# Cached keys of a decoder layer: from TensorE transposes in the attention to VectorE transposes during the projections

## What is computed

```python
xn = rmsnorm(x, norm_mix_pre)
q, k, v, u_a, v_a = project(xn, w_in)              # 4 heads; k and q are 2 x 64 per head
pk = cache_k[l][page_table]                        # 8 sequences x 8 pages x 128 keys x 4 heads x 128
pv = cache_v[l][page_table]
o_b = diff_head_out(attend(q, k, v, lam), ...)     # softmax(q1 k1) - lam * softmax(q2 k2), both + bias
o_a, vn = spatial_gate(u_a, v_a, ...)              # u * (W_s LayerNorm(v) + b) in chunks of 128
x = x + rmsnorm(concat(o_b, o_a) @ w_out, norm_mix_post)
f, new_buf = conv_ffn(rmsnorm(x, norm_ffn_pre), ...)
x = x + rmsnorm(f, norm_ffn_post)
```

## Time and profile before

| | before |
|---|---|
| median of 3 runs (lowest to highest) | 1375.17 us (1374.22 to 1375.6) |
| profiled execution, span of its trace | 1374.4 us |
| PE busy | 1351.8 us |
| DVE busy | 703.4 us |
| ACT busy | 461.7 us |
| projections | 46 to 282.3 us |
| attention | 282.3 to 457.2 us |

### The profile page before, as it was taken

One profiled execution on the slowest core, in us unless ns is written; L12 is line 12 of the kernel. 1 busy time (PEld: TensorE's weight loads), 2 busy tenths in 40 slices (PEclk: granted clock), 3 DMA queues, 4 the chain that ended last, 5 costly groups with the idle time before them and its releaser, 6 DMA issues.

```text
span 1374.4 us, 22383 instructions
## 1 busy us (share of the span) xinstructions
PE 1351.8 (98%) x8642; PEld 1216.2 (88%) x8642; DVE 703.4 (51%) x1175; ACT 461.7 (34%) x783; POOL 169.7 (12%) x323
## 2 busy tenths in 40 slices
PE   7999999999999999999999999999999999999998
PEld 6999999966667788899898989898989898999986
DVE  6333412166778564554545464646364545364555
ACT  6321012056666643343131313132313232322332
POOL 2254000021212221120000000000000000000003
PEclk9999999999999999999999999999999999999999
DMA  8202123256673633132020202011111102020117
GB/s 267 63 31 66 31 70 104 76 178 187 197 209 146 221 103 120 54 108 77 16 76 15 76 15 70 22 61 31 61 31 40 52 15 76 15 73 19 47 47 134
DMA packets 93658, 113.43 MB, mean 83 GB/s; under 512 B 6477, under 2 KB 65526, under 8 KB 93590
## 3 DMA queue, kind: packets, MB, share of 16 engines
q1 hardware_dynamic: 90457, 105.52, 24.5%
q0 software_dynamic: 992, 3.54, 1.6%
q10 hardware_dynamic: 2140, 3.46, 0.7%
HBM read 97.28 MB, written 14.69 MB: 81 GB/s over the span
## 4 chain that ended last, share of the span: by engine, by line
PE 93%; DVE 2%; issue 1%; ACT 1%; DMA 1%; SPq 1%; POOL 0%; POOLq 0%; DVEq 0%; ACTq 0%
PE PS L2383 38%; PE PS L2094 17%; PE PS L2448 16%; PE PS L2326 7%; PE PS L2187 2%; PE PS L2149 2%; PE PS L2210 2%; PE PS L2463 2%; PE PS L2478 2%; DMA x_in<-in_x_prompt_dram 1%; PE PS L2256 1%; PE PS L2233 1%; PE PS L2079 1%; PE PS L2317 1%; PE PS L2175 1%
## 5 line engine op out<-in xcount | busy, mean ns | idle before, releaser
L2383 PE MATMUL PS<-act_lo,wu_hi 128*128 128x364 f32 (+1 forms) x1056 | 346.5, 328 | 0.0
L2383 PE MATMUL PS<-act_hi,wu_lo 128*128 128x364 f32 (+1 forms) x1056 | 346.1, 328 | 0.0
L2383 PE MATMUL PS<-act_hi,wu_hi 128*128 128x364 f32 (+1 forms) x1056 | 346.0, 328 | 0.0
L2383 PEld LDWEIGHTS PS<-act_hi,wu_hi 128*128 128x128 f32 x1056 | 198.6, 188 | 0.5
L2383 PEld LDWEIGHTS PS<-act_lo,wu_hi 128*128 128x128 f32 x1056 | 198.2, 188 | 0.4
L2383 PEld LDWEIGHTS PS<-act_hi,wu_lo 128*128 128x128 f32 x1056 | 198.4, 188 | 0.0
L1854 DVE TENSOR_TENSOR y_acc<-y_acc,PS 128x512 f32<-128x512 f32 x162 | 111.1, 686 | 116.1 <-PE PS L2448 116.1
L2448 PE MATMUL PS<-wd_hi,g_hi 128*128 128x512 f32 x324 | 130.2, 402 | 0.0
L2448 PE MATMUL PS<-wd_lo,g_hi 128*128 128x512 f32 x324 | 128.0, 395 | 0.0
L2448 PE MATMUL PS<-wd_hi,g_lo 128*128 128x512 f32 x288 | 114.0, 396 | 0.0
L1239 ACT CAST g_hi<-conv 128x1088 fp32r<-128x1088 f32 x21 | 23.1, 1102 | 245.8 <-PE PS L2448 189.7
(11 more groups left out here) (286 smaller groups left out, 2371.4 us busy)
## 6 DMA issues: line engine op xcount, KB each, us to landing
wu_raw<-in_w_up_dram SPq DMA_DIRECT2D x44, 512.0 KB, 3.9
vpage<-in_cache_v_dram SPq DMA_DIRECT2D x64, 256.0 KB, 3.0
kpage<-in_cache_k_dram SPq DMA_DIRECT2D x60, 256.0 KB, 3.0
wd_raw<-in_w_down_dram SPq DMA_DIRECT2D x22, 512.0 KB, 5.3
w_raw<-in_w_in_dram SPq DMA_DIRECT2D x20, 512.0 KB, 4.7
x_in<-in_x_prompt_dram SPq DMA_DIRECT2D x8, 512.0 KB, 7.8
wo_raw<-in_w_out_dram SPq DMA_DIRECT2D x8, 512.0 KB, 6.0
x_res<-in_x_prompt_dram SPq DMA_DIRECT2D x8, 512.0 KB, 4.4
```

What stands on the lines that cost most here:

```text
L2383: mm = nc.tensor.matmul(PS[:, 3 * half + c, 0:kept(c)], a[:, half, k, :], b[:, k, KEPT[c]], start=(j == 0), stop=(j == len(parts) - 1))
```

## The change

- Pages of keys are loaded two at a time (a pair, 32 of them) during the projections, by SP, into one of two places (k_tok0, k_tok2). SP waits for the turn that freed the place.
- DVE turns a pair with one instruction in 32 x 32 blocks into k_tok1 (`turn_pair`, L1542), after the pair is loaded and after all earlier pairs have been stored (there is one k_tok1).
- ACT issues the store of k_tok1 to a DRAM tensor keys_t, 4 KB from each partition (`store_pair`, L961). It waits for the turn.
- Seven sets of 5, 5, 5, 5, 5, 4 and 3 pairs are spread over the jobs of groups va1 to q1. A set's loads stand in SP's queue behind the weights of the group after the one in which it is turned.
- In the attention SP loads units of turned keys (four DMAs each, of 32 partitions, in runs of 1 KB) into kt directly, in three places and one first place. `turn_key` and both `take_keys` are gone; `smp_scores` reads its keys and writes its scores in runs of 32.
- The page table is loaded at the start; some semaphores are shared.

```diff
+    PAIR_SETS = [range(0, 5), range(5, 10), range(10, 15), range(15, 20), range(20, 25), range(25, 29), range(29, 32)]
+    TOK_OF = [2 * (n % 2) if n < 25 else 0 for n in range(NPAIR)]
+    PAIR_AT = [jobs_of(k + 1)[j * len(jobs_of(k + 1)) // len(pairs)] for k, pairs in enumerate(PAIR_SETS) for j in range(len(pairs))]
...
+        def load_pair(n):
+            b = TOK_OF[n]
+            if tok_uses(n):
+                sp.wait_ge(ktok_turned, max(m for m in range(n) if TOK_OF[m] == b) + 1)
+            else:
+                sp.wait_ge(nrm_ready, STEPS)
+            for a in range(2):
+                at_page = page_index(n // 2, 2 * (n % 2) + a)
+                page = sp.value_load(pages[0:1, at_page:at_page + 1], min_val=0, max_val=n_pool - 1)
+                sp.dma_start(k_tok[b][:, a, :], cache_k[0, bass.ds(page, 1)].rearrange("a t h d -> t (a h d)")).then_inc(slot_loaded[b], 16)
...
         for p in range(4, 2 * len(GROUPS)):
             sp.wait_ge(w_lo_ready, p - 1)
             load_w(sp, p)
+            if p % 2 == 1 and p // 2 - 2 < len(PAIR_SETS):
+                for n in PAIR_SETS[p // 2 - 2]:
+                    load_pair(n)
...
         def load_keys(u):
-            pr, c, b2 = unit(u)
-            for p in range(4):
-                n = 4 * u + p
-                if n >= 8:
-                    sp.wait_ge(kturn_ready, n - 7)
-                at_page = NPAGE * (2 * pr + b2) + 4 * c + p
-                page = sp.value_load(pages[0:1, at_page:at_page + 1], min_val=0, max_val=n_pool - 1)
-                sp.dma_start(kpage[u][:, p, :], cache_k[0, bass.ds(page, 1)].rearrange("a t h d -> t (a h d)")).then_inc(kp_loaded[u % 2], 16)
+            if u == 1:
+                sp.wait_ge(kt_loaded[0], 64)
+            if u >= 4:
+                sp.wait_ge(sscore_ready, 2 * (u - 3) + 2)
+            for j in range(4):
+                src = bass.AP(keys_t, (2 * u * 4 * 32 * 4 + j) * 256, [[4 * 256, 32], [32 * 4 * 256, 8], [1, 256]])
+                dst = kt[u][32 * j:32 * j + 32].rearrange("a n i p h t -> a (n i) (p h t)")
+                sp.dma_start(dst, src).then_inc(kt_loaded[kt_place(u)], 16)
...
+        def store_pair(n):
+            act.wait_ge(ktok_turned, n + 1)
+            dst = keys_t[n].rearrange("i d j c -> (i d) (j c)")
+            act.dma_start(dst, k_tok[1][:].rearrange("p a c -> p (a c)")).then_inc(ktok_stored, 16)
...
             if kind in ON_ACT and n >= STEPS:
                 take_job(n)
+            if n in PAIR_AT:
+                store_pair(PAIR_AT.index(n))
...
+        def turn_pair(n):
+            b = TOK_OF[n]
+            dve.wait_ge(slot_loaded[b], 48 + 32 * (tok_uses(n) + 1))
+            if n >= 1:
+                dve.wait_ge(ktok_stored, 16 * n)
+            blocks = k_tok[b][:].rearrange("p a (h j c) -> p j (a h) c", h=H, c=32)
+            turned = k_tok[1][:].rearrange("p a c -> p (a c)").rearrange("p (j n t) -> p j n t", j=4, t=32)
+            nc.vector.transpose(turned, blocks).then_inc(ktok_turned, 1)
...
             if n == len(jobs) - 1:
                 ahead()
+            if n in PAIR_AT:
+                turn_pair(PAIR_AT.index(n))
             if kind in ON_ACT:
                 continue
...
         def smp_scores(j):
-            for i in range(2):
-                pe.wait_ge(kt_ready[i], j + 1)
+            pe.wait_ge(kt_loaded[kt_place(u)], 64 * ((u - 1) // 3 + 1 + (kt_place(u) == 0)))
...
             for h in range(H):
-                mm = nc.tensor.matmul(PS[32 * h:32 * h + 32, SMP_BANK, ks], qp[:, 2 * pr + b2, h, :], kt[:, u % 2, h, ks],
+                out = PS[32 * h:32 * h + 32, SMP_BANK, ks].rearrange("r (p i t) -> r i p t", p=2, t=32)
+                mm = nc.tensor.matmul(out, qp[:, 2 * pr + b2, h, :], kt[u][:, j % 2, :, :, h, :],
                                       start=(j % 4 == 0), stop=(j % 4 == 3))
...
-            for n in keys_of(i):
-                turn_key(n)
```

More of the change, by code:

```diff
@@ L142, in _program @@
     far_min = keep.put("far_min", [P, 4, 2])
-    keep.put("spare", [P, P - 8])
+    pages = keep.put("pages", [1, NB * NPAGE], I32)
+    keep.put("spare", [P, P - 8 - NB * NPAGE])
     gain = keep.put("gain", [P, D])
@@ L238, in _program @@
     lo_place = Region(ACT_BYTES, 2 * ACT_BYTES)
-    kt = lo_place.put("kt", [P, 2, H, 512])
-    kpage1 = lo_place.put("kpage1", [P, 4, 512])
+    kt_a, kt_b, kt_mid = (lo_place.put(n, [P, 2, 4, 2, H, 32]) for n in ("kt_a", "kt_b", "kt_mid"))
     prob0 = lo_place.put("prob0", [P, 2, SEQ])
@@ L333, in own_step @@
         eng.wait_ge(step, steps[id(step)])
-    x_loaded = [sem(f"x_loaded{i}") for i in range(3)]
+    slot_loaded = [sem(f"slot_loaded{i}") for i in range(3)]
     gain_loaded = sem("gain_loaded")
@@ L514, in _program @@
     sbias_loaded = sem("sbias_loaded")
[L515 removed]
     sel_loaded = sem("sel_loaded")
[L517 to L518 removed]
+    ktok_turned = sem("ktok_turned")
+    ktok_stored = sem("ktok_stored")
+    kt_loaded = [sem(f"kt_loaded{i}") for i in range(3)]
     vp_loaded = [sem(f"vp_loaded{i}") for i in range(2)]
@@ L609, in unit, with page_index @@
         return u // 4, u // 2 % 2, u % 2
+    def page_index(u, p):
+        pr, c, b2 = unit(u)
+        return NPAGE * (2 * pr + b2) + 4 * c + p
     SMP_BANK, AT_BANK, PV_BANK, OWN_BANK = 7, 1, 3, 6
@@ L617, in _program, with jobs_of, tok_uses, kt_place @@
     ZERO_STEP = [8, 16, 28, 32]
-    def keys_of(i):
-        return range(2 * i, 2 * i + 2) if i < 2 else range(4, 8) if i == 2 else range(2 * i + 2, min(2 * i + 4, 4 * 2 * NB))
+    NPAIR = NB * NPAGE // 2
+    PAIR_SETS = [range(0, 5), range(5, 10), range(10, 15), range(15, 20), range(20, 25), range(25, 29), range(29, 32)]
+    TOK_OF = [2 * (n % 2) if n < 25 else 0 for n in range(NPAIR)]
+    def jobs_of(g):
+        return [n for n, job in enumerate(jobs) if job[1] == g]
+    PAIR_AT = [jobs_of(k + 1)[j * len(jobs_of(k + 1)) // len(pairs)] for k, pairs in enumerate(PAIR_SETS) for j in range(len(pairs))]
+    def tok_uses(n):
+        return TOK_OF[:n].count(TOK_OF[n])
+    def kt_place(u):
+        return max(u - 1, 0) % 3
     ring, ring_taken = [], []
@@ L1747, in _ @@
                     out_norm(i - 3)
-            for n in keys_of(i):
-                if n % 2 == 1 and n not in (3, 5):
-                    take_keys(n)
             if i == 0:
@@ L2202, in turn_out @@
             mm.then_inc(ot_ready, 1)
-        def turn_key(n):
-            u, p = n // 4, n % 4
-            if p == 0:
-                pe.wait_ge(kp_loaded[u % 2], 64 * (u // 2 + 1))
-            pe.wait_ge(*ring_free("key", n))
-            for h in range(H):
-                mm = nc.tensor.transpose(PS[:, ring_bank("key", n), P * h:P * h + P], kpage[u][:, p, P * h:P * h + P], ident[:])
-            mm.then_inc(kturn_ready, 1)
         def own_scores():
```

87 lines of the change are left out of this document (31 added, 56 removed).

## The result

The changed kernel takes 1406.93 us (median of 4 runs, 1405.57 to 1408.69) against 1374.76 before (median of 4, 1374.22 to 1375.6); the ratio is 1.0232, 95% interval 1.0219 to 1.0244. It is slower by 32 us, where I had forecast 15.

The account below looks back on a forecast made before the run. PE was taken as the bound, busy in 1351.8 of 1374.4 us. Stalls of 29.6 us in the projections less 15.0 gained in the attention gave +14.6, hence 1390 us, range 1370 to 1410.

Parts of the forecast that it names:

- case B: Rival, chance 0.18: worse than 1376 to 1402; period near 5.6 us or more (1400), or the clock falls (1402 to 1412).
- case A: The forecast itself, chance 0.56: chain delays PE by 16 to 35 us, attention gives 11 to 20; 1376 to 1402.
- The turn and the period: Projections' chain: 1.2 us a turn on DVE; with hand-overs, store landing and load contention 5.0 us a pair, bounds 4.0 to 5.6.
- The idle time of the projections: PE stalls from turns and stores: 17.2 us up to k0, 7.2 by job 38, 5.2 before krow; 29.6 in sum.
- the granted clock under full after the stalls: Sign listed as showing the prediction wrong: PE's clock below its higher level after stalls; nothing for it in the sum.
- The attention's 15.0 us: Gain in the attention from dropping PE's transposes of cached key pages: 15.0 us summed by step, bounds 11 and 20.
- steps 0 to 3: First narrow attention steps: gain 2.8 us, four times 1.02 less 1.3 for the later-requested second unit of keys.
- Steps 8 to 11: Narrow attention steps: gain 3.5 us, after 1.1 lost because sample scores wait for the softmax of the scores before.
- 16 to 19: Narrow attention steps: the same 3.5 us gain as in steps 8 to 11.
- the wide ones: Wide attention steps 20 to 27, paced by a loop of DVE and ACT: gain about 1.1 us.
- C: Rival, chance 0.14: faster, the projections' chain costs less than the attention gives; 1368, or 1358 to 1371.
- D: Rival, chance 0.12: attention becomes bound by its key loads to 32 partitions, losing part of its gain; 1395 to 1400.

Follow-up runs that it names:

- experiment 3: Changed kernel with the turns of pairs 5 to 9 moved inside DVE's LayerNorm rounds instead of behind them; 1387.71 us, ratio 1.0095 to the kernel before.
- experiment 6: Changed kernel with sets of 5, 8, 0, 5, 5, 5, 4 pairs, the 8 turned inside the LayerNorm rounds; 1377.24 us, ratio 1.0007 to the kernel before.
- experiment 9: experiment 7 with the second loading place usable up to pair 29 and sets of 5, 8, 0, 6, 5, 6, 2; 1365.75 us, ratio 0.9927.
- experiment 5: Changed kernel storing only half of each turned pair (2 KB from each partition); 1396.90 us, ratio 1.0156 to the kernel before.
- experiment 4: Changed kernel with turned pairs going to two places in turn up to pair 24, each with its own semaphore; 1387.29 us, ratio 1.0086 to the kernel before.
- Experiment 8: experiment 1 with the second unit of keys given its own place and requested earlier, as in experiment 7; 1363.64 us, ratio 0.9912 to the kernel before.
- experiment 2: experiment 1 with each key load going to all 128 partitions, 2 KB each, instead of 32 partitions, 8 KB each; 1366.72 us, ratio 0.9931.
- experiment 7: experiment 6 with the second unit of keys given its own place and requested at the last projection group's first job; 1374.15 us, ratio 0.9987.
- experiment 1: Changed kernel with no pair loaded, turned or stored in the projections; attention loads cache blocks as they lie; 1367.01 us, ratio 0.9932 to the kernel before.

## Why the prediction was wrong, point by point

The direction was right and its mechanism too; the size was off by a factor of two, because one term was left out of the sum and one mis-sized. The sum said +14.6 us and the traces show +31.9. Of the 17.3 between, 9.7 are busy time of PE behind the stalls that the sum had at nothing, 7.2 are missing from the attention's gain, and 0.4 is idle time. The range of 1370 to 1410 held 1407 only by the half of case B that it took in; case A's own, 1376 to 1402, did not.

**The turn and the period: right.** 1.24 us for a turn (1.2 taken), 5.14 us a pair (5.0 taken). The parts were not quite: most stores land in 2.8 to 3.1, and the 0.7 that I spread over every pair is a single landing of 6 to 7 us in a set, beside the weights. The "11 percent" of the period in which DVE runs was wrong: 1.2 of 5.0 us is 24.

**The idle time of the projections: right.** 29.6 us worked out, 30.0 measured, at the places named: job 27 7.4 (5.7 forecast), k0 10.0 (11.5), jobs 37 and 38 6.5 (7.2), krow 6.2 (5.2), and none in q0, q1 and v. That the sum is right to 0.4 us is in part luck, since its terms miss by 0.7 to 1.7 in both directions; and nearly half of the third, the wait of 3.1 before job 37, ended with ACT's copy of the last u job, not with the key copy that I had traced. Experiments 3, 6 and 9 moved the turns, and most of the waits went, experiment 5 gave the slope.

**The price of the stalls in clock: left out of the sum.** I had it only as rival B, for one job behind each of three stalls, up to 12 us; it belonged in the forecast, since the forecast itself made the gaps. Measured: 9.7 us more of busy time, 8.8 of it the clock. The term is "29.6 us", which should have been 39.3. "TensorE: Matmul & The Clock Gate" of the Trainium skill, section "Why this matters for your kernels", had warned of idle gaps, and the trace now agrees: the granted clock is 0.94 over the projections, with rows of 0.50 us a matmul behind four of the stalls. A run that keeps PE busy through its stalls was not tried, so this split of the loss rests on the trace, while experiments 3, 4 and 9 show only that clock and stalls go together (0.987, 0.989 and 0.994 over their spans, 0.981 for the change). The prediction named "the granted clock under full after the stalls" among the signs that it was wrong, and it is the sign that came, with PE's wait for keys.

**The attention's 15.0 us: mis-sized, 7.8 measured.** By the starts of DVE's mixing in each step, before and after, the delay goes from 37.5 us at step 0 to 41.8 at step 2, 38.5 at step 11, 36.9 at step 19, 35.9 at step 24 and 32.05 at step 31. So steps 0 to 3 did not give 2.8: 2.2 are gained ahead of the first mixing (39.7 at the end of the projections, 37.5 there) and 3.6 lost behind it. The wait of 4.5 us for the second unit did that, where I had allowed 1.3; its unit is requested at 322.9 and used at 331.1, 8.2 us later and not 6, with two more units requested right behind it. Steps 8 to 11 gave 2.4 (3.5 forecast), 16 to 19 1.2 (3.5), 28 to 31 3.7 (4.1), and the wide ones 1.9 in all (1.1). Experiment 8 puts what the wait cost at 2.8 to 3.4 us and leaves 11 to 12 of the 15. The wait for the sample exponential is the one that I had named for the middle blocks, at the price that I had named (1.05 us). What I had not counted is the clock behind it in step 16: from the start of the products to the first transpose behind them PE takes 3.82 us there (405.24 to 409.06) and 2.59 in step 8 (362.21 to 364.80). That is the 1.2 us by which steps 16 to 19 gave less than 8 to 11. The 1.1 us by which both blocks fall short besides may stand in waits that the kernel before does not have: PE waits for o_nrm, that is for DVE, 0.97 and 0.90 us in steps 11 and 12, and the same in 19 and 20:

```profile
380.12 0.68 PE L2210 MATMUL PS<-v_all,at_sb 128*128 128x128 f32 x4 [0.97 <-DVE o_nrm L1584]
...
384.22 0.91 PE L2210 MATMUL PS<-v_all,at_sb 128*128 128x128 f32 x6 [0.90 <-DVE o_nrm L1584]
```

I had taken it that PE sets the pace in narrow steps with the transposes gone as with them. No run separates these waits, so this last part stays open.

**The rivals.** B's mechanism happened, its long period did not. C was wrong: nowhere near. D's mechanism shows in the landings (experiment 2), but PE waits for keys at one place only, where it is worth 1.9 us of wait, and nothing that the total shows. `smp_scores` costs what it did at the higher clock, 0.64 us for the eight records of a step, so runs of 32 cost nothing. A's range is not the sum of its own bounds: 16 to 35 us less 20 to 11 is 1371 to 1399, not 1376 to 1402; the measured time lies outside either.

Open: experiments 6 and 7 varied by 8 us from run to run, where others vary by 2 to 6; why was not looked into.

## What to carry to other kernels

A helper chain through a single buffer (turn, store, wait, turn) costs its period times the jobs that stand in order behind it, however idle the engine looks: place it where that engine waits anyway (here inside rounds that wait for POOL), not between two stages, and count the loading place too. Price a stall of TensorE as the stall plus what runs at the lower clock behind it, here 1.8 to 1.9 us behind each stall of 6 to 10 us that stood alone and 3.3 behind the two of 3.1 and 3.3 us in close succession. And when a first load is requested later than before, work out its landing with the loads queued right behind it, not with the median.

## What was not expected of the hardware

- Stalls of 3.3 to 10.0 us of PE were each followed by 3.8 to 5.9 us of work at 1.2 GHz; the length of the stall made little difference (3.80 us behind 7.4, 3.81 behind 10.0, 3.92 behind 6.2). The clock had fallen before the stall of 7.4 us was over: it is 0.80 in the mean of that stall.
- The length of a short wait does not tell whether the clock falls. Waits of 2.56 us (experiment 4) and 2.91 (experiment 9) were followed by 3.6 and 3.2 us at 1.2 GHz, one of 2.55 (experiment 6) and one of 1.01 (experiment 3) by none. Of two waits of 1.05 us in the changed kernel one was followed by the lower clock and the other not.
- At 1.2 GHz the matmuls of 128 x 364 started 0.303 us apart instead of 0.167, so half the clock took 1.8 times as long and not twice.
- A store of 512 KB that mostly lands in 2.8 to 3.1 us takes 6.0 to 7.2 beside 1 MB of weights and a pair's load, while a load of weights takes 6.3 (4.7 before).
- Loads of 256 KB to 32 partitions each land in 5.7 us in the median (experiment 1, kt_a, 270 to 330 us), over 128 partitions in 3.9 (experiment 2).
